# A two-layer decoder step on one core: cached values in pairs, pages ahead of weight blocks, six turned-key buffers, and query parts in a row

## What is computed

```python
def mixer_sublayer(x, pos, conv_ctx, lp, past):
    hn = rms_norm(x, lp["norm_mix_pre"])
    a, b_glu, g_conv, q_lat, kv_lat, k_pe, g_mla = split_in_proj(hn, lp["w_in"])
    ...
    q = jnp.einsum("bsr,rhe->bshe", rms_norm(q_lat, lp["q_norm_g"]), lp["w_uq"])
    ...
    if past is None:
        attn = mla_prompt_attention(q_nope, q_pe, c_kv, k_pe, lp["w_uk"], lp["w_uv"])
    else:
        attn = mla_sample_attention(q_nope, q_pe, c_kv, k_pe, past[0], past[1], lp["w_uk"], lp["w_uv"])
    mla_out = attn * jax.nn.silu(g_mla)
    y = jnp.einsum("bsc,cd->bsd", jnp.concatenate([conv_out, mla_out], axis=-1), lp["w_out"])
    x = x + rms_norm(y, lp["norm_mix_post"])
    return x, c_kv, k_pe, u_ext[:, -CONV_STATE:]

def memory_kv(mem, lp):
    mn = rms_norm(mem, lp["norm_mem"])
    mem_k = jnp.einsum("bmd,dhe->bmhe", mn, lp["w_mk"])
    mem_v = jnp.einsum("bmd,dhe->bmhe", mn, lp["w_mv"])
    return mem_k, mem_v

def cross_sublayer(x, mem_k, mem_v, lp):
    hn = rms_norm(x, lp["norm_x_pre"])
    q = jnp.einsum("bsd,dhe->bshe", hn, lp["w_xq"])
    s = jnp.einsum("bshe,bmhe->bhsm", q, mem_k).astype(jnp.float32) * MEM_SCALE
    p = jax.nn.softmax(s, axis=-1).astype(mem_v.dtype)
    o = jnp.einsum("bhsm,bmhe->bshe", p, mem_v)
    y = jnp.einsum("bshe,hed->bsd", o, lp["w_xo"])
    return x + rms_norm(y, lp["norm_x_post"])
```

## Time and profile before

| | us |
|---|---|
| median of 3 runs (lowest, highest) | 1190.46 (1188.66, 1192.6) |
| profiled execution | 1187.28 |
| its span, first to last instruction | 1185.6 |
| TensorE busy | 1133.7, 96% |
| VectorE busy | 894.6, 75% |
| ScalarE busy | 643.4, 54% |
| GpSimd busy | 172.8, 15% |
| mean granted TensorE clock | 0.994 of full |
| moved by DMA | 216 MB, mean 182 GB/s |

### The profile page before, as it was taken

One profiled execution on the slowest core, in us unless ns is written; L12 is line 12 of the kernel. 1 busy time (PEld: TensorE's weight loads), 2 busy tenths in 40 slices (PEclk: granted clock), 3 DMA queues, 4 the chain that ended last, 5 costly groups with the idle time before them and its releaser, 6 DMA issues. The chain is left out here.

```text
span 1185.6 us, 25819 instructions
## 1 busy us (share of the span) xinstructions
PE 1133.7 (96%) x10203; PEld 1058.5 (89%) x10203; DVE 894.6 (75%) x1530; ACT 643.4 (54%) x1130; POOL 172.8 (15%) x282
## 2 busy tenths in 40 slices
PE   6999999999999999999879999999999999999988
PEld 6999999999777899997869999999997779999877
DVE  5789998899867544687587999889998674448856
ACT  7474454645557444565665644454545664446554
POOL 1210101010353000032011010101014520001310
PEclk9999999999999999999989999999999999999999
DMA  7795746475668466687347767564754765667852
GB/s 211 189 268 139 223 131 182 132 190 137 168 190 243 141 184 182 184 259 271 116 113 197 212 162 203 151 179 129 193 153 143 231 202 148 184 189 213 279 195 74
DMA packets 318971, 216.13 MB, mean 182 GB/s; under 512 B 21620, under 2 KB 300512, under 8 KB 318298
## 3 DMA queue, kind: packets, MB, share of 16 engines
q1 hardware_dynamic: 301728, 164.64, 50.4%
q0 software_dynamic: 16800, 49.83, 13.3%
q10 hardware_dynamic: 330, 0.11, 0.0%
HBM read 209.31 MB, written 7.15 MB: 183 GB/s over the span
## 5 line engine op out<-in xcount | busy, mean ns | idle before, releaser
L1327 ACT ACTIVATE whi<-stage 128x2048 fp32r<-128x2048 f32 (+2 forms) x157 | 272.9, 1739 | 272.6 <-PE U L691 228.7
L1950 DVE TENSOR_TENSOR wlo<-stage,whi 128x2048 fp32r<-128x2048 f32 x138 | 315.8, 2289 | 129.2 <-ACT whi L1327 129.1
L689 PE MATMUL U<-Ahi,whi 128*128 128x264 f32 x1152 | 331.7, 288 | 1.2 <-DVE wlo L1950 0.5
L690 PE MATMUL U<-Alo,whi 128*128 128x264 f32 x1152 | 326.6, 284 | 0.0
L691 PE MATMUL U<-Ahi,wlo 128*128 128x264 f32 x1152 | 326.1, 283 | 0.0
L689 PEld LDWEIGHTS U<-Ahi,whi 128*128 128x128 f32 x1152 | 217.1, 188 | 3.7 <-DVE wlo L1950 1.6
L690 PEld LDWEIGHTS U<-Alo,whi 128*128 128x128 f32 x1152 | 217.2, 189 | 0.0
L691 PEld LDWEIGHTS U<-Ahi,wlo 128*128 128x128 f32 x1152 | 216.2, 188 | 0.0
L2127 DVE SCALAR_TENSOR_TENSOR acc<-uext,cwall,acc 128x256 f32<-128x256 f32 x464 | 189.3, 479 | 0.4
L689 PE MATMUL U<-Bhi,whi 128*128 128x264 f32 x384 | 108.9, 284 | 0.0
L690 PE MATMUL U<-Blo,whi 128*128 128x264 f32 x384 | 108.8, 283 | 0.0
(11 more groups left out here) (462 smaller groups left out, 2171.3 us busy)
## 6 DMA issues: line engine op xcount, KB each, us to landing
stage<-in_w_in SPq DMA_DIRECT2D x76, 1024.0 KB, 6.0
stage<-in_w_out SPq DMA_DIRECT2D x32, 1024.0 KB, 5.9
stage<-in_w_mk SPq DMA_DIRECT2D x8, 1024.0 KB, 6.2
cp<-in_cache_kv_latent POOLq DMA_DIRECT2D x64, 128.0 KB, 3.2
cp<-in_cache_kv_latent SPq DMA_DIRECT2D x64, 128.0 KB, 2.9
stage<-in_w_mv SPq DMA_DIRECT2D x8, 1024.0 KB, 5.4
Kt<-in_cache_mem_k POOLq DMA_DIRECT2D x16, 512.0 KB, 5.9
stage<-in_w_xq SPq DMA_DIRECT2D x8, 1024.0 KB, 7.0
```

The source lines that it names most:

```text
L689: mm(bk[:, 0:cols], whi[:, s, w], hi[:, k, :], start=(k == 0), stop=False)
L690: mm(bk[:, 0:cols], whi[:, s, w], lo[:, k, :], start=False, stop=False)
L1327: return A_(out, in_, ACT.Copy, scale=scale)
L1950: ins = V.tensor_tensor(wlo[:, s, :], stage[:, s, :], whi[:, s, :].bitcast(F32), ALU.subtract)
```

## The change

Seven edits, all to the order of work, to buffers or to waits; every product, copy and transfer of before is still made.

1. **Cached values two at a time.** `vm_load` becomes a pair, taken in turn in the order of loading (6, 0, 1, 2, 3, 4, 5, 7). From the third block on GpSimd waits, before it issues a value block, for the landing of the one two places before: values 4 waits for 2, 5 for 3, 7 for 4.
2. **Output weight block 1 behind the values.** SyncE waits for all value landings of the layer before it loads it; the blocks behind it wait with it.
3. **Keys earlier.** Key blocks 4 and 5 are loaded behind the seventh row store, 6 and 7 behind the eighth, and no longer behind ScalarE's copy of the fourth query block. `KTB` has six buffers in place of four, so VectorE turns blocks 4 and 5 without waiting for scores.
4. **Scores joined.** `y_scores(4)` to `y_scores(7)` stand in a row; `x_values(2)` follows behind `x_transposes(3)`, and `x_values(3)` stands behind the value products (L1253). VectorE's `x_out(2)` and `x_out(3)`, ScalarE's `x_upper(2)` and `x_upper(3)` move back with them: `x_upper(2)` and the copy of output weight block 1 now come behind the exponent `dX` and directly ahead of the table load. TensorE waits for the fourth head only at the last piece of the first output block.
5. **Query parts in a row.** The four parts of the first query block come one after the other, with `mem_rows(7)` behind the first, and then the four groups of column sums. On ScalarE `mem_out(5)` moves ahead of its step and the copy of query block 1 behind `raw_upper(8, 3)`.
6. **Pages ahead of weight blocks.** On SyncE pages 4 come ahead of memory-key block 3, pages 6 ahead of output block 0, pages 7 ahead of output block 1.
7. **The last page group's exponent.** ScalarE does `d_exp(7)` and `d_alpha(7)` ahead of `ln_upper(6)`.

The diff, without most of its context lines:

```diff
@@ -219,7 +219,7 @@
...
     Kt = [at(f"Kt{b}", [P, 2, MH * MD], KTO[b]) for b in range(NB)]
-    KTB = [at(f"KTB{e}", [P, 2, 16, 32], o) for e, o in enumerate((A0 + 16384, A0 + 20480, W + 37632, W + 33536))]
+    KTB = [at(f"KTB{e}", [P, 2, 16, 32], o) for e, o in enumerate((A0 + 16384, A0 + 20480, W + 37632, W + 33536, B1 + 8192, B1 + 12288))]
...
@@ -311,7 +311,7 @@
...
     km_load = [S(f"km_load{e}") for e in range(4)]
-    vm_load = S("vm_load")
+    vm_load = [S(f"vm_load{e}") for e in range(2)]
...
@@ -393,6 +393,9 @@
...
 
+    def key_slot(b):
+        return KTB[b % 6]
+
...
@@ -470,13 +473,13 @@
...
             load_pages(sp, l, 3, 0)
+            load_pages(sp, l, 4, 0)
             load_mk(3)
-            load_pages(sp, l, 4, 0)
             load_pages(sp, l, 5, 0)
+            load_pages(sp, l, 6, 0)
             load_out(0)
-            load_pages(sp, l, 6, 0)
+            load_pages(sp, l, 7, 0)
             load_out(1)
-            load_pages(sp, l, 7, 0)
...
@@ -489,6 +492,9 @@
...
             for j in range(4):
+                if j == 1:
+                    for e in range(2):
+                        sp.wait_ge(vm_load[e], 64 * (l + 1))
...
@@ -584,31 +590,32 @@
...
             def load_values(b):
-                pool.dma_start(Vt[b][:, :, :], mv_d[:, ds(l * 2 + b * 2 * L, 2), :]).then_inc(vm_load, 16)
+                pool.dma_start(Vt[b][:, :, :], mv_d[:, ds(l * 2 + b * 2 * L, 2), :]).then_inc(vm_load[(6, 0, 1, 2, 3, 4, 5, 7).index(b) % 2], 16)
...
                     load_keys((0, 2, 4, 5).index(s))
+                if s == 6:
+                    load_keys(4)
+                    load_keys(5)
...
             store_rows(2 * MH - 1)
-            load_values(6)
+            load_keys(6)
+            load_keys(7)
...
             nc.gpsimd.memset(qm[:, :, :, :, :], 0.0).then_inc(m_zero.sem, 1)
-            for b in range(2):
-                wait_apart(pool, kb_rdy.sem, kb_rdy.at(l, b + 1))
-                load_values(b)
-            wait_apart(pool, split_hi.sem, split_hi.at(l, U_XQ + 4))
-            for b in range(4, NB):
-                load_keys(b)
-            for b in range(2, 4):
-                wait_apart(pool, kb_rdy.sem, kb_rdy.at(l, b + 1))
-                load_values(b)
-            wait_apart(pool, unit_done.sem, unit_done.at(l, U_XQ + 4))
-            nc.gpsimd.memset(pm[:, :, :, :, :], 0.0).then_inc(m_zero.sem, 1)
-            for b in (4, 5, 7):
+            load_values(6)
+            for k, b in enumerate((0, 1, 2, 3, 4, 5, 7), 1):
+                if b < 4:
+                    wait_apart(pool, kb_rdy.sem, kb_rdy.at(l, b + 1))
+                if b == 4:
+                    wait_apart(pool, unit_done.sem, unit_done.at(l, U_XQ + 4))
+                    nc.gpsimd.memset(pm[:, :, :, :, :], 0.0).then_inc(m_zero.sem, 1)
+                if k >= 2:
+                    wait_apart(pool, vm_load[k % 2], 16 * (4 * l + k // 2))
...
@@ -1148,10 +1155,11 @@
...
                 part(U_XQ, 0, Bhi[:, :, :], Blo[:, :, :], 4 * q, 4 * q + 4)
+                if q == 0:
+                    mem_rows(7)
+            for q in range(4):
...
                 last = group([yg[:, 4 * q + c, :] for c in range(4)], q == 0, q == 3)
-                if q == 0:
-                    mem_rows(7)
...
@@ -1201,7 +1209,7 @@
...
                     for h in range(MH):
-                        last = mm(ST[32 * h:32 * h + 32, 0:64], qm[:, eb, h, b, :], KTB[b % 4][:, :, 4 * h + eb, :],
+                        last = mm(ST[32 * h:32 * h + 32, 0:64], qm[:, eb, h, b, :], key_slot(b)[:, :, 4 * h + eb, :],
...
@@ -1228,12 +1236,11 @@
...
             y_scores(4)
-            x_values(2)
...
             y_scores(6)
+            y_scores(7)
             x_transposes(3)
-            y_scores(7)
-            x_values(3)
+            x_values(2)
...
@@ -1246,13 +1253,15 @@
...
             pe.wait_ge(ym_dve.sem, ym_dve.at(l, YM_PROBS))
-            pe.wait_ge(vm_load, l * (16 * NB) + 16 * NB)
+            for e in range(2):
+                pe.wait_ge(vm_load[e], 64 * (l + 1))
...
             last.then_inc(yo_mm.sem, 1)
+            x_values(3)
...
@@ -1273,6 +1282,8 @@
...
                     for k in range(MH):
+                        if bl == 0 and k == MH - 1:
+                            pe.wait_ge(xv_ev.sem, xv_ev.at(l, MH))
...
@@ -1757,9 +1768,9 @@
...
             ln_upper(5)
-            ln_upper(6)
...
             d_alpha(7)
+            ln_upper(6)
...
@@ -1809,16 +1820,21 @@
...
             for s in range(4):
+                if s == 3:
+                    mem_out(5)
...
                 copy(mvT[:, s % 2, :], U[s % 2][:, 0:NM]).then_inc(u_evac.sem, 1)
-                hi(U_MV + s + 2, s)
-                mem_out((0, 2, 3, 5)[s])
+                if s < 3:
+                    hi(U_MV + s + 2, s)
+                    mem_out((0, 2, 3)[s])
...
                 raw_upper(8, s, Bhi, G_XPRE, par)
+                if s == 3:
+                    hi(U_MV + s + 2, s)
...
@@ -1880,19 +1896,19 @@
...
             x_scaled(3)
-            x_upper(2)
-            hi(U_XO + 1, 1)
...
                ).then_inc(yex.sem, 1)
-            x_upper(3)
+            x_upper(2)
+            hi(U_XO + 1, 1)
...
             copy(XOhi[:, :, TP:T], HC[:, 256:384].rearrange("p (h x) -> p h x", x=32)[:, :, 0:NB]).then_inc(xo_hi.sem, 1)
+            x_upper(3)
...
@@ -2543,13 +2559,13 @@
...
                         dve.wait_ge(st_mk[e], l * 64 + 32)
-                if b >= 4:
-                    dve.wait_ge(ys_mm.sem, ys_mm.at(l, b - 3))
-                V.transpose(KTB[b % 4][:, :, :, :].rearrange("p t c a -> p (t c a)"),
+                if b >= 6:
+                    dve.wait_ge(ys_mm.sem, ys_mm.at(l, b - 5))
+                V.transpose(key_slot(b)[:, :, :, :].rearrange("p t c a -> p (t c a)"),
...
             def x_out(h):
-                dve.wait_ge(xo_hi.sem, xo_hi.at(l, h + 1))
+                dve.wait_ge(xo_hi.sem, xo_hi.at(l, h + 1 + h // 3))
...
@@ -2571,17 +2587,16 @@
...
             x_query(3)
+            key_blocks(4)
...
             x_max(2)
-            key_blocks(4)
+            key_blocks(5)
...
             x_out(1)
-            key_blocks(5)
+            key_blocks(6)
...
             x_recip(3)
-            key_blocks(6)
-            x_out(2)
...
@@ -2598,13 +2613,14 @@
...
                           HC[:, 0:64].rearrange("p (t h b) -> p t h b", t=2, h=MH)).then_inc(ym_dve.sem, 1)
-            x_out(3)
...
             V.reciprocal(sm[0:R, 11:12], U[1][0:R, P + 2:P + 3]).then_inc(ym_dve.sem, 1)
+            x_out(2)
             lo(U_XO + 1, 1)
-            dve.wait_ge(xo_hi.sem, xo_hi.at(l, MH + 1))
+            dve.wait_ge(xo_hi.sem, xo_hi.at(l, MH))
...
                             XOhi[:, :, TP:T].bitcast(F32), ALU.subtract).then_inc(xo_lo.sem, 1)
+            x_out(3)
...
```

## The result

The changed kernel takes **1201.07 us** (median of 6 runs, 1199.82 to 1202.34); beside it the kernel before took 1188.94 (6 runs). The ratio is 1.0099, 95% interval 1.0087 to 1.0111: 12 us slower, where the prediction said 1191.8 with 1187.5 to 1197.5. The profiled execution took 1202.34 us, at the upper end of its runs, and its span is 1200.7, against 1187.28 and 1185.6. So the two traces differ by 15 us and the medians by 12.

A forecast was written before the change was run, and what follows sets the result against it. TensorE, busy 96% of the span, bounds the kernel; only some 50 us of pauses can be won. Chain +3.35, pages -1.25, exponent -0.8 sum to +1.3 us: 1188.6 profiled, 1191.8 as median, range 1187.5 to 1197.5.

The forecast's parts named there:

- The chain: Cross-attention stage: values 2, 4, 7, weight block 1, copy, table, doX delay the first output-weight product; +1.95 and +1.4, sum +3.35 us.
- The rule that decides: Cross-attention stage: ScalarE's copy order, SyncE's wait for values and GpSimd's two in flight together set the first output-weight product.
- T - M: From the first turn of the memory's keys (M) to the first product with the output weights (T); forecast times 565.6 and 1148.2.
- Value block 2's issue: Start of the value loads: shift between -1.3 and 0 us against before, middle of -0.6 taken.
- Three landings and two wakes: Values 2, 4, 7 land one after another at 4.0 us each, plus two GpSimd wakes of 0.6: 13.2 us.
- The weight block: Output weight block 1, issued by SyncE once all values are in: lands 5.0 us later.
- rival (a): TensorE's clock falls in the new pause of about 4 us before doX: 1.4 us per layer, time 1194.6; chance 0.24.
- Pages ahead of weight blocks: Layer 0, SyncE's page order: TensorE's 1.25 us wait for a page goes, -1.25 us, in that layer alone.
- Rival (d): Output weight block 0 comes late in both layers and page groups wait for ScalarE: +2.8 us, 1193.3; chance 0.10.
- The exponent: Last page group: exponent first shortens TensorE's 0.62 us wait for sD; -0.4 per layer, -0.8 us in all.
- Query parts in a row: First query block: 1.3 us gained per layer, reaching the first output-weight product only through value block 2, counted there.
- Rival (c): Output weight block 1 does not gate doX; TensorE's own chain decides: -6.5 us, time 1184.0; chance 0.08.

The follow-up runs named there:

- the two runs that cut it at either end: Changed kernel without SyncE's wait for the values before output weight block 1: 1187.84 us; changed kernel with both copies of that block behind doX: 1189.45 us.
- keys late: Changed kernel with key blocks 4 to 7 issued at the place they had before: 1200.36 us.
- 8 and 20 idle products: Changed kernel with 8 (layer 0) and 20 (layer 1) idle identity products in TensorE's pause before doX is turned: 1198.7 us.
- before with the gate: Kernel before, with SyncE holding output weight block 1 for all eight values and ScalarE copying it directly ahead of the table load: 1193.64 us.
- before with query parts in a row: Kernel before, with only the query parts in a row and the two ScalarE shifts that belong to them: 1186.55 us.
- the three kernels with the copies behind doX: Changed kernel with output weight block 1's copies behind doX: 1189.45 us; also with keys 4 to 7 late, without GpSimd's landing waits 1185.3, with them 1187.35.
- the one without pacing: Changed kernel without GpSimd's wait for the landing two places back; SyncE still waits for all values: 1192.84 us.
- the kernel before with the three small edits: Kernel before, with SyncE's page order, the last exponent ahead of ln_upper(6), and query parts in a row with two ScalarE shifts: 1185.75 us.
- the run without the gate: Changed kernel in which SyncE does not wait for the value landings before output weight block 1: 1187.84 us.
- gated best version with pacing: Changed kernel with keys 4 to 7 late and output weight block 1's copies behind doX; GpSimd's and SyncE's waits stay: 1187.35 us.

## Why the prediction was wrong

**Which steps failed.** Two, in terms of the prediction's sum. The chain was costed too short: T later by 3.35 us in the two layers together, where the traces show 10.8. And the lower clock behind the new pause stood in the sum with nothing, where it cost 4.95. The rest of the change was to give back 2.05 and gives back 0.65. That is 15.1 us between the traces in place of 1.3.

**The rule that decides: right.** The prediction's chain (value 2, value 4, value 7, weight block 1, copy, table, doX, T) is the chain of the trace, and the two runs that cut it at either end give everything back. GpSimd waits for landings, SyncE for the values, ScalarE for the block, as it said.

**The size of the chain: wrong, in three terms.** It gave T - M of 71.2 in each layer (565.6 - 494.43 and 1148.2 - 1077.04). The three kernels that have both waits and the copy ahead of doX (the changed one, keys late, 8 and 20 idle products) show 72.9 to 76.9 in six stretches, 74.4 on the mean (the idle products have a part of 1 us in one of them).

- *Value block 2's issue.* Taken as 0.6 us earlier than before; it came 1.9 and 1.5 later, at M + 50.7 and 50.3 in place of 48.8. This is the chain's largest miss, 2.5 and 2.1 us. It differs between executions: in the seven kernels with the keys early it is from 1.1 us earlier than before to 2.4 later, 0.9 later on the mean, so the changed kernel's profile shows a bad case and the typical miss is 1.5. The prediction saw that a block that shares the engines can take 9.0 us in place of 5.0 and that ScalarE and VectorE would be held up, and then took the middle between -1.3 and 0, as if the end of the range were no delay. Query weight block 3 took 9.9 us and output weight block 0 11.4 (layer 0). VectorE, layer 0, turns key blocks 2 and 3 and only then frees TensorE with qX:

```profile
543.08 2.36 DVE L2564 STREAM_TRANSPOSE KTB<-Kt 128x1024 f32<-128x1024 f32 x2
545.37 0.39 DVE L2526 TENSOR_TENSOR qX<-U,rs 128x264 f32<-128x264 f32 x1
```

  Its part of the query parts' gain was there (TensorE reached this place 1.1 us earlier), and the pause ate it.
- *Three landings and two wakes*, 13.2 us: 12.5 and 15.2 in the changed kernel, 13.0 and 13.5 in the one with 8 and 20 idle products. Value 2 lands in 3.5 and 3.9 us, better than the 4.0 taken, but from the second landing that is waited for to the next issue it is 1.1 us and not 0.6, and value 7 took 3.6 in one layer and 5.2 in the other. The Trainium skill, DMA: Bandwidth & Descriptors, section Anatomy of one DMA, led to an estimate of 3.2 us for such a block; no landing here reaches it, the shortest is 3.5, against the 3.8 us that was the shortest row shown of before.
- *The weight block*, 5.0 us alone: here it goes out together with block 2, whose place had long been free, and takes 5.0 and 6.6 us (5.1 to 6.6 in the other kernels with the gate).

The links behind it were right: 4.7 us from the copy's start to T, 72.9 - 68.2 and 76.9 - 72.1, against 1.9 + 1.5 + 1.3.

**The clock: rival (a), under-rated twice.** It came about in both layers. It had a chance of 0.24 on the ground that 4 us is less than half of 9.4, and a price of 1.4 us a layer. The clock fell behind pauses of 2.41 and 5.61 us, and its price was 2.8 and 2.15 us. The price went wrong because the prediction counted the 3.3 busy us of the one stretch of the earlier trace rows; here the products run at 0.22 us in place of 0.12 for 4.8 us behind T in layer 1, and for longer in layer 0. It also fell behind the first pause, 2.71 us (0.76 in the first stretch shown). The Trainium skill, TensorE: Matmul & The Clock Gate, section Why this matters for your kernels, advises against long idle gaps between bursts of products; the pause of 5.61 us agrees, and here the clock fell behind shorter ones too. With the measured terms in the prediction's own sum, T later by 5 us twice (the mean of the six stretches), 5 for the clock, pages and exponent 1.3 back, it comes to +13.7; measured are 12.1.

**Pages ahead of weight blocks: half right.** The wait of 1.25 us at its place is gone in every kernel with the new order and still there, 1.80 and 1.81 us, in the two without (before with the gate, before with query parts in a row). But in the changed kernel a wait of the same kind stands 36 us later, at the last page group, where a weight block is now issued 0.4 us behind the pages:

```profile
382.13 1.06 PE L910 MATMUL HAB<-ident,cp 128*128 128x128 f32 x8 [1.27 <-issue]
```

In the other kernels with the new order it was from 0 (in the three kernels with the copies behind doX, among others) to 1.92 us, and 1.83 in layer 1 of the one without pacing. So of the forecast's -1.25 about half is left, as an estimate. Rival (d), output block 0 late, is 0.70 us of ScalarE's wait in the changed kernel and reached nobody; in the kernel before with the three small edits ScalarE waited 2.98 us for that block, and TensorE 1.10 us behind it for sD. (The prediction speaks of both layers there and counts its 1.5 us once.)

**The exponent: right.** The wait of 0.62 us for sD is gone, and 0.22 to 0.23 stand behind VectorE's copy: 0.4 a layer, as forecast.

**Query parts in a row: right** in size (1.2 and 0.9 of 1.3 us on the kernel before). In the changed kernel nothing of it arrives.

**Rival (c)**, the block does not gate, did not come about; the run without the gate shows what it would have been, 1187.8 and not 1184: the paced values then hold TensorE for 1.7 to 1.8 us, and in layer 1 the clock costs it 1.7 more.

## What to carry to other kernels

Before a transfer is made to wait for others, look at the engine that will consume it, and at what stands behind that consumer in its order: a block that nobody wants for 6 us cost 12 us because a small step on the critical path was queued behind its copy. When a chain of landings is costed, put its start at the crowded end of the range, and add the clock to every new pause as a term of the sum and not as a rival.

## What was not expected of the hardware

- The granted clock fell behind pauses of TensorE from 1.29 to 5.61 us in this sparse stage, and did not fall behind others of up to 2.90 us (layer 1 of the gated best version with pacing; 2.43 and 2.46 in two more). Behind 1.29 us (the kernel before with the gate, layer 1) it took 6.82 us to the fourth group in place of 5.24; in its layer 0, behind 1.44, it took 4.47. The length of the pause does not decide by itself. In the trace of before, a stop of 9.4 us was the only case until the kernel's end.
- A weight block of 1024 KB landed in 5.0 us alone, in 9.9 beside four key blocks (query weight block 3), in 11.4 beside four key blocks and two value blocks (output weight block 0), and in 13.4 in the crowd of the kernel before (output weight block 2), with no harm there, since its copy came late enough.
- One execution's pause ahead of the masked query was 2.71 us, another's of the same instructions 0.19 or 0.84: such a wait can't be read from one profile.
- Stops of TensorE of 0.4 to 2.5 us inside a run of 128 small products, always at the same product of a given order, each ending 1.2 to 1.6 us behind a 16 KB transfer of instructions.
